# One transformer block on one core: the first attention layer in two halves of heads, its scores and softmax placed between pieces of the QKV and output products

## The chip, the core and the metric

One core of a Trainium2 chip runs the whole program. The metric is the device time of one execution in microseconds (us). Engines are named as the profile names them: PE is the matrix engine, DVE the vector engine, ACT the scalar engine, POOL the general one, SP the engine that here only issues DMAs. 1 MB is a million bytes.

## The reference, cut to what matters

Batch 1, 256 latent tokens and 256 context tokens, width 1024, everything in float32. The first layer is differential attention over 8 heads:

```python
sh1, sc1, g1, sh2, sc2, g2 = split(silu(c) @ w_mod[i] + b_mod[i], 6)     # 6 x 1024 columns, for two layers
hx, hc = x * (1 + sc1) + sh1, ctx * (1 + csc1) + csh1                    # csh1, csc1 from c_ctx
q, k, v = hx @ w_q, concat(hc, hx) @ w_k, concat(hc, hx) @ w_v           # w_qkv is 1024 x 3072
q, k_latent = rope(q), rope(k_latent)
p[h, m] = softmax(q[h, m] @ k[h, m].T / 8)                               # 8 heads, m = 0, 1, 256 queries x 512 keys
o[h] = (p[h, 0] - lam * p[h, 1]) @ v[h]                                  # 128 wide
y = (rms(o[h]) * subln_g * (1 - lam_init)) @ w_o                         # 1024 x 1024
x = layer_norm(ALPHA * x + g1 * y)
x = layer_norm(ALPHA * x + g2 * swiglu(x * (1 + sc2) + sh2))             # "ffn0": 1024 x 5632, 2816 x 1024
```

A second layer (pooling, then "ffn1") and a third block ("z", three sparse attentions, "ffn2") follow. The change doesn't touch what they compute.

## The kernel before, in words

**Weight panels.** All big weights go through one list, `w_panels` (L124): pieces of 512 rows by 512 columns, 1.05 MB each. SP issues the DMA of panel i into a ring of four slots (L1873 to L1882) once panel i-4 has been used (`sp.wait_ge(*done[i - RING])`). To reach float32 accuracy each panel is split: ACT writes its rounded high part (`split_hi`, L858) into one of two buffers, so it must wait until panel i-2 has been used, and DVE writes the low part (`split_lo`, L1114). `split_to(n)` on either engine works through the panels up to n, in order. PE then makes three products for each tile (high by high, high by low, low by high; `product`, L493).

The order is qkv (12 panels, 0 to 11), wo (12 to 15), ffn0_in (16 to 37, two for each of 11 column blocks "nb"), ffn0_out (38 to 49), pool (50), ffn1_in (51 to 72), and so on.

**The modulation.** `w_mod` is two layers of 1024 x 6144. The kernel takes it in 24 pieces ("events") of 512 columns, 2.1 MB each, into two buffers of `aux` (`mod_panel`, L389). Events 0 to 3 (shift and scale of the first layer, needed at once) are made on PE as 8 products of 2 columns by 512. Events 4 to 23 are made on DVE (`mod_product`, L1195): one tensor_scalar and seven scalar_tensor_tensor of 128x512 each, and PE only sums over partitions (`mod_reduce`). `mod_acc` counts finished DVE events. The DMA of event e overwrites the buffer of event e-2, so SP waits for `mod_acc` before it issues it. SP is one queue: a panel DMA that stands behind such a wait waits too. Where the mod DMAs stand among the panels is worked out in L1869 to L1872:

```python
at = min(event_panel[e - 4] + (5 if e < 16 else 7), event_panel[e - 2] + 3)
```

In ffn0_in there are six events for 11 column blocks (`FFN_EVENTS`: nb 1, 3, 5, 7, 9, 10), and four in ffn0_out (`OUT_EVENTS`).

**First attention layer.** (1) Prologue: constants, 16 small loads and the table, all on SP's queue; the four PE events; transposes of x. (2) QKV in six column blocks (`gemm`, L512), 2 or 4 token tiles each, Q and K by tokens; DVE turns Q and K by the rope tables in four instructions for each tile (L1253 to L1258). The transposes and the modulation of the context stand behind the first block. (3) Q and K are transposed by PE and copied back (L537, L911, L1267). (4) 16 units (token tile, head): two score products (K = 64 each, two row halves of the array), maxima on DVE (two reductions and a scaling, L1273, L1275), two exponentials on ACT (L924), mixing on DVE (four instructions, L1282 to L1289), four transposes on PE, a copy on ACT (L933), four value products on PE. Three units are in flight. (5) Norm of the heads, eight transposes, the wo product (four groups of 24 tiles' products), then residual and LayerNorm (`residual_stats`, L1332; `normalise`), and ffn0.

**In ffn0_in**, DVE does for block nb: low part of panel p(nb,0)+2, the second half of an event of nb-1, low part of p(nb,1)+2, then multiply, round and subtract for the block's activations, then finish an event and start the next (L1424 to L1446).

## Time and profile before

| what | us |
|---|---|
| median of 3 runs | 1356.54 (1355.19 to 1358.63) |
| the profiled execution's own time | 1360.89 |
| its span, first to last instruction | 1359.1 |
| PE busy / DVE busy / ACT busy | 1197.0 / 851.9 / 493.5 |
| first QKV product starts | 63.6 |
| first ffn0_in product starts | 311.6 |
| mean granted PE clock | 0.947 of full |

All times in a trace count from the span's start. The profiled execution took 4.4 us more than the median, 1.8 us of it outside the span. "Idle before, with a releaser" is time in which an engine stood still, and the thing whose semaphore ended it. A busy share says little by itself: PE's ends are modelled, and each stage has its own limit.

### The profile page before, as it was taken

Reading aid. Unit: us, or ns where it says so; the run is one execution under the profiler, and the core shown is the slowest. Engines: PE = TensorE matmul, PEld = TensorE weight load, DVE = VectorE, ACT = ScalarE, POOL = GpSimd, SP = SyncE. Lnnn points to the kernel's source line nnn. Section 1 sums busy time; section 2 is a strip of 40 time slices with the busy share of each in tenths; the row PEclk is TensorE's granted clock in tenths of the full one; section 3 lists DMA queues with packets and bytes.
Section 4 is the critical chain, followed back from the end, with each engine's and each line's share of the span. In section 5 each row is a group of like instructions: output and inputs, shape, how many; then the busy total and the mean of one; then the engine's idle time right before and its main releaser. Section 6 shows DMA issues by size and latency. Waiting matters only on the chain.

```text
span 1359.1 us, 17055 instructions
## 1 busy us (share of the span) xinstructions
PE 1197.0 (88%) x6927; PEld 1006.6 (74%) x6927; DVE 851.9 (63%) x1304; ACT 493.5 (36%) x688; POOL 90.3 (7%) x33
## 2 busy tenths in 40 slices
PE   4779997679999887799999699949999898899998
PEld 0257775469999675699987598847787646799977
DVE  0388858866878877755554665767856425555543
ACT  0232226534333222333333445524444333433332
POOL 0000000000000000000000002321224200000000
PEclk9889999999999898799999799968889999899999
DMA  6967687154887674485555356511122244455553
GB/s 214 361 229 266 229 294 167 32 201 125 274 291 254 236 263 136 133 288 184 181 175 173 107 182 202 155 32 63 34 73 80 79 138 153 126 185 182 180 181 109
DMA packets 155758, 236.77 MB, mean 174 GB/s; under 512 B 4901, under 2 KB 86178, under 8 KB 155554
## 3 DMA queue, kind: packets, MB, share of 16 engines
q1 hardware_dynamic: 150068, 223.36, 49.4%
q10 hardware_dynamic: 5614, 12.33, 3.3%
q8 instruction: 55, 0.90, 0.3%
q14 instruction: 21, 0.17, 0.0%
HBM read 229.12 MB, written 6.55 MB: 173 GB/s over the span
## 4 chain that ended last, share of the span: by engine, by line
PE 69%; DVE 12%; issue 9%; ACT 4%; DMA 3%; POOL 1%; SPq 1%; POOLq 0%; DVEq 0%; ACTq 0%
PE bank L493 66%; PE bank L537 3%; ACT w_hi L858 2%; DVE ring_lo L1114 2%; DMA ring<-in_ffn_w_in 2%; DVE small L1273 1%; DVE modacc L1211 1%; POOL small L1807 1%; DMA aux<-in_w_mod 1%; SPq L1861 1%; POOL ring_lo L1798 1%; DVE y_tok L1352 1%; DVE small L1355 1%; DVE small L1682 1%; DVE y_tok L1349 1%
## 5 line engine op out<-in xcount | busy, mean ns | idle before, releaser
L1114 DVE TENSOR_TENSOR ring_lo<-ring,w_hi 128x2048 fp32r<-128x2048 f32 (+4 forms) x142 | 314.0, 2213 | 304.7 <-ACT w_hi L858 304.6
L858 ACT ACTIVATE w_hi<-ring 128x2048 fp32r<-128x2048 f32 (+4 forms) x154 | 285.9, 1858 | 560.7 <-PE bank L493 547.1
L493 PE MATMUL bank<-h_hi,w_hi 128*128 128x256 f32 x1056 | 303.2, 287 | 2.9 <-DVE h_lo L1133 1.9
L493 PE MATMUL bank<-h_lo,w_hi 128*128 128x256 f32 x1056 | 299.9, 284 | 0.0
L493 PE MATMUL bank<-h_hi,ring_lo 128*128 128x256 f32 x1056 | 299.7, 284 | 0.0
L493 PEld LDWEIGHTS bank<-h_hi,w_hi 128*128 128x128 f32 x1056 | 203.9, 193 | 5.5 <-issue 5.5
L493 PEld LDWEIGHTS bank<-h_lo,w_hi 128*128 128x128 f32 x1056 | 203.8, 193 | 1.7 <-issue 1.7
L493 PEld LDWEIGHTS bank<-h_hi,ring_lo 128*128 128x128 f32 x1056 | 203.8, 193 | 0.0
L493 PE MATMUL bank<-w_hi,h_hi 128*128 128x512 f32 (+4 forms) x416 | 168.7, 405 | 15.1 <-ACT big L906 4.8
L493 PE MATMUL bank<-ring_lo,h_hi 128*128 128x512 f32 (+4 forms) x416 | 164.7, 396 | 0.0
L493 PE MATMUL bank<-w_hi,h_lo 128*128 128x512 f32 (+4 forms) x416 | 164.0, 394 | 0.0
L493 PE MATMUL bank<-w_hi,ff_hi 128*128 128x512 f32 x264 | 105.3, 399 | 13.8 <-DVE ring_lo L1114 13.7
L493 PEld LDWEIGHTS bank<-w_hi,h_hi 128*128 128x128 f32 x416 | 82.1, 197 | 35.9 <-issue 18.9
L1211 DVE SCALAR_TENSOR_TENSOR modacc<-aux,cs,modacc 128x512 f32<-128x512 f32 x140 | 105.2, 752 | 4.8
L493 PE MATMUL bank<-big 128*128 128x128 f32 (+5 forms) x386 | 88.3, 417 | 20.3 <-ACT big L933 11.2
L493 PE MATMUL bank<-ring_lo,ff_hi 128*128 128x512 f32 x264 | 104.4, 396 | 0.0
L493 PE MATMUL bank<-w_hi,ff_lo 128*128 128x512 f32 x264 | 104.3, 395 | 0.0
L493 PEld LDWEIGHTS bank<-w_hi,h_lo 128*128 128x128 f32 x416 | 81.8, 197 | 16.0
L493 PEld LDWEIGHTS bank<-ring_lo,h_hi 128*128 128x128 f32 x416 | 81.9, 197 | 14.6 <-issue 0.2
L493 PEld LDWEIGHTS bank<-big 64*128 64x128 f32 (+2 forms) x386 | 55.3, 209 | 46.1 <-issue 26.0
L1807 POOL TENSOR_TENSOR small<-small,neghalf 128x2 f32<-128x2 f32 (+1 forms) x11 | 16.8, 1531 | 873.7 <-DVE small L1360 481.3
L537 PE MATMUL bank<-table,y_tok 128*128 128x128 f32 x128 | 26.3, 371 | 50.8 <-DVE y_tok L1374 27.3
(202 smaller groups left out, 1385.5 us busy)
## 6 DMA issues: line engine op xcount, KB each, us to landing
aux<-in_w_mod SPq DMA_DIRECT2D x24, 2048.0 KB, 10.0
ring<-in_ffn_w_in SPq DMA_DIRECT2D x88, 512.0 KB, 4.9
ring<-in_w_in SPq DMA_DIRECT2D x24, 1024.0 KB, 5.0
ring<-in_w_ffn_in SPq DMA_DIRECT2D x44, 512.0 KB, 4.7
ring<-in_ffn_w_out SPq DMA_DIRECT2D x20, 1024.0 KB, 5.2
ring<-in_attn_w_qkv SPq DMA_DIRECT2D x12, 1024.0 KB, 12.0
ring<-in_w_ffn_out SPq DMA_DIRECT2D x10, 1024.0 KB, 5.1
bias_rows<-srow ACTq DMA_DIRECT2D x1, 5376.0 KB
```

Of the source, the lines that this page charges most:

```text
L493: return nc.tensor.matmul(o, l, r, start=start, stop=stop, **kw)
L537: ins = nc.tensor.transpose(bank[0:src.shape[1], i * P:i * P + src.shape[0]], src, ident[0:src.shape[0], 0:src.shape[0]])
L858: nc.scalar.activation(panel_part(i, 0), raw_panel(i), ACT.Copy).then_inc(w_hi, 1)
L1114: V.tensor_tensor(panel_part(i, 1), raw_panel(i), panel_part(i, 0).bitcast(F32), ALU.subtract)\
L1211: ins = V.scalar_tensor_tensor(acc, w[:, j, :], c, acc, ALU.mult, ALU.add)
L1273: step(V.tensor_reduce(small[:, s + 4 + m:s + 5 + m], result(dve, ("S", u, m))[:, :], AX, ALU.max))
L1349: empties(V.tensor_tensor(y, result(dve, (stage, nb, tt))[:, :], gate[:, sl], ALU.mult), (stage, nb, tt))
L1352: step(V.scalar_tensor_tensor(y, x_tok[:, tt, sl], ALPHA, y, ALU.mult, ALU.add))
L1355: step(V.bn_stats(st, y))
L1682: V.tensor_scalar(small[:, o:o + 3], small[:, o + 8:o + 11], 0.1 * NEG, -1.0, ALU.max, ALU.mult)\
L1798: nc.gpsimd.tensor_tensor(panel_part(i, 1), raw_panel(i), panel_part(i, 0).bitcast(F32), ALU.subtract).then_inc(w_lo_mix, 1)
L1807: nc.gpsimd.tensor_tensor(dst, src, exponent, ALU.pow).then_inc(rstd_done, 1)
```

## The change

QKV runs as K, Q, V of heads 0 to 3, then K, Q, V of heads 4 to 7 (`QKV_ORDER`). K and Q are made transposed (weights as the stationary operand, 512 or 256 tokens moving), so their 48 transposes fall away; the rope's swap of halves becomes a product with a permutation (`swap`), and DVE turns two heads at once with three instructions. Latent and context tokens are modulated together in 512-wide chunks, the first four chunks ahead of the first product, the other four inside it. Scores of heads 0 to 3 stand between the value pieces, their transposes and value products between the K pieces of heads 4 to 7; those of heads 4 to 7 between pieces of wo. Maxima are one reduction over two banks, mixing three instructions. The four PE events use `cs[:, 2j:2j+32]` and write to four groups of 32 output partitions. The small loads move to ACT's queue. The remaining modulation is 20 halves (4 of 8 rows of a whole 1024-column component, 2.1 MB each): six in the attention, one in each of ffn0_in's blocks nb 0 to 9, two in ffn0_out, two in ffn1_in. The DMA of half m waits for products 0 to m-2 and stands ahead of panel 2m+6 for m = 8 to 15. The store of the bias rows (5.5 MB, ACT's queue) moves from behind QKV into the prologue, and the load of the bias from ffn1_in's block 2 to block 6.

```diff
+QKV_ORDER = (2, 0, 4, 3, 1, 5)
...
-    for nb in range(6):
+    for nb in QKV_ORDER:
         for kg in range(2):
             add(("qkv", nb, kg), a["attn_w_qkv"][0], kg, PK, nb * NB, nb * NB + NB)
-    for nb in range(2):
-        for kg in range(2):
+    for kg in range(2):
+        for nb in range(2):
...
+        modhalf = [v3(aux[:, 4096 * i:4096 * i + 4096], KC // 2) for i in range(MODS)]
...
-        turn = {"gemm": 0, "misc": 0, "unit": 0, "mix": 0}
-        POOLS = {"gemm": (0, 1, 2, 3, 4, 5), "misc": (6, 7), "unit": (0, 1, 2, 3, 4), "mix": (5,)}
+        POOLS = {"gemm": (0, 1, 2, 3, 4, 5), "misc": (6, 7), "unit": (0, 1, 2, 3, 4), "mix": (5,),
+                 "dense": (0, 1, 2, 3), "pre": (4, 5, 6, 7), "score": (4, 5, 6, 7), "out": (4, 5)}
...
+        FIRST = (0, 2, 1, 3)
+        N_FIRST, N_HALVES = 4, 20
+        def mod_first_panel(eng, n):
+            if n >= MODS:
+                result(eng, ("modrow", n - MODS))
+            e = FIRST[n]
+            eng.dma_start(modring[n % MODS], a["w_mod"][0, :, e * NB:(e + 1) * NB]
+                          .rearrange("(p j) n -> p j n", j=KC)).then_inc(mod_landed[n % MODS], 16)
+        def mod_half_panel(eng, m):
+            if m < MODS:
+                result(eng, ("modrow", N_FIRST - MODS + m))
+            else:
+                eng.wait_ge(mod_acc, m - MODS + 1)
+            l, comp = divmod(2 + m // 2, 6)
+            j0 = (m % 2) * (KC // 2)
+            rows = a["w_mod"][l, :, comp * D:(comp + 1) * D].rearrange("(p j) n -> p j n", j=KC)
+            eng.dma_start(modhalf[m % MODS], rows[:, j0:j0 + KC // 2, :]).then_inc(mod_landed[m % MODS], 16)
+        def mod_is_row(comp):
+            return comp in (2, 5, 6, 7, 8, 11)
+        HALF_AT = {("ffn0", nb): [6 + nb] for nb in range(10)}
+        HALF_AT.update({("ffn0_out", 0): [16], ("ffn0_out", 1): [17], ("ffn1", 1): [18], ("ffn1", 2): [19]})
+        COMP_AT = {("ffn0", 2): 5, ("ffn0", 4): 6, ("ffn0", 6): 7, ("ffn0", 8): 8, ("ffn0", 10): 9, ("ffn1", 4): 11}
...
+            def mod_rows_first(n):
+                pe.wait_ge(mod_landed[n % MODS], 16 * (n // MODS + 1))
+                bank = take(("modrow", n), "pre")
+                for j in range(KC):
+                    q = 32 * (j % 4)
+                    ins = mm(bank[q:q + 32, :], cs[:, 2 * j:2 * j + 32], modring[n % MODS][:, j, :], j < 4, j >= 4)
+                fills(ins, ("modrow", n))
...
+            def swap_keys(pr):
+                for h in (2 * pr, 2 * pr + 1):
+                    wait_emptied(pe, ("K", h))
+                pe.wait_ge(turn_landed, 16)
+                fills(mm(v3(take(("swapK", pr), "misc"), 2), swap, kT[:, 2 * pr:2 * pr + 2, SEQ:], True, True), ("swapK", pr))
...
+            def keys_and_queries(hg, between):
+                for kg in range(2):
+                    for j in range(4):
+                        keys(hg, kg, j)
+                        between(4 * kg + j)
+                queries(hg, 0)
+                between(8)
+                swap_keys(2 * hg)
+                swap_keys(2 * hg + 1)
+                queries(hg, 1)
+            def values_and_scores(hg):
+                vals(hg, 0, 0)
+                swap_queries(2 * hg)
+                swap_queries(2 * hg + 1)
+                if hg == 0:
+                    mod_sums(2)
+                vals(hg, 0, 1)
+                for u in range(6):
+                    scores(8 * hg + u)
+                    vals(hg, (u + 2) // 4, (u + 2) % 4)
+                for u in (6, 7):
+                    scores(8 * hg + u)
...
+            def first_columns(i):
+                if i == 1:
+                    for n in (2, 3):
+                        mod_rows_first(n)
+                if i == 2:
+                    for n in (2, 3):
+                        mod_columns_first(n)
+                    for ch in range(PK, KC):
+                        tokens(ch)
+                if i == 3:
+                    wait_emptied(pe, ("pre", KC - 1))
+            def first_heads(i):
+                if 1 <= i <= 8:
+                    values(i - 1)
+                if i < 8:
+                    turn_probs(i)
+                if i == 8:
+                    mod_sums(3)
+            wait_emptied(pe, ("pre", PK - 1))
+            keys_and_queries(0, first_columns)
+            values_and_scores(0)
+            keys_and_queries(1, first_heads)
+            values_and_scores(1)
...
+            o_transposes(0)
+            turn_probs(8)
+            turn_probs(9)
+            wait_emptied(pe, ("oT", 1))
+            wo(0, 0, 0)
+            values(8)
+            for u in range(9, 12):
+                turn_probs(u + 1)
                 values(u)
-
-
-            pe.wait_ge(o_done, 4)
-            for h in range(HEADS):
-                transposes(("oT", h), [y_tok[:, tt, h * P:(h + 1) * P] for tt in range(TT)])
+            wo(0, 0, 1)
+            for u in range(12, 16):
+                if u < 15:
+                    turn_probs(u + 1)
+                values(u)
+            wo(1, 0, 0)
+            mod_sums(4)
+            wo(1, 0, 1)
+            o_transposes(1)
+            wait_emptied(pe, ("oT", 3))
             for nb in range(2):
-                gemm("wo", lambda tt, c: token_tile(hT, c, tt), range(TT), nb, NB, HALVES,
-                     inputs=lambda c: (("oT", c),))
+                for tt in range(TT):
+                    wo(nb, 1, tt)
...
+            act.dma_start(table[:, :], a["const_table"]).then_inc(table_landed, 16)
+            for dst, src in small_loads:
+                act.dma_start(dst, src).then_inc(cols_landed, 16)
+            act.dma_start(lam_in, a["attn_lambda"][0].partition_broadcast(P)).then_inc(lam_landed, 16)
+            act.dma_start(big[:, 11776:12160], a["const_turn"]).then_inc(turn_landed, 16)
...
+            def scores_out(hg):
+                first = panel_at[("qkv", 4 + hg, 0)]
+                for u in (0, 1):
+                    exps(8 * hg + u)
+                split_to(first + 2)
+                for u in (2, 3):
+                    exps(8 * hg + u)
+                for tt in range(4):
+                    value_copy(hg, tt)
+                    if tt == 3:
+                        split_to(first + 3)
+                    exps(8 * hg + 4 + tt)
+            split_to(2)
+            for h in range(4):
+                key_copy(h)
+            split_to(4)
+            query_copy(0)
+            query_copy(1)
+            split_to(5)
+            scores_out(0)
+            for u in range(3):
+                probs_copy(u)
+            split_to(8)
+            probs_copy(3)
+            key_copy(4)
+            squares(0)
+            probs_copy(4)
+            key_copy(5)
+            probs_copy(5)
+            key_copy(6)
+            probs_copy(6)
+            key_copy(7)
+            split_to(9)
+            probs_copy(7)
+            split_to(10)
+            squares(1)
+            query_copy(2)
+            query_copy(3)
+            split_to(11)
+            scores_out(1)
+            o_highs(0)
+            for u in range(8, 12):
+                probs_copy(u)
+            squares(2)
+            split_to(14)
+            for u in range(12, 16):
+                probs_copy(u)
+            squares(3)
+            bias_row(g2row, 0, 5, g_landed[5])
+            for r, w in enumerate(("ln_g", "ln_b")):
+                row_load(ln_rows[:, r, :], a[w][0, 0, :], ln_landed)
+            split_to(15)
+            o_highs(1)
...
+            def mod_product(m, js=range(KC // 2)):
...
+                w = modhalf[m % MODS]
                 for j in js:
+                    jj = (m % 2) * (KC // 2) + j
+                    c = cs[:, 2 * jj:2 * jj + 1]
+                    if jj == 0:
+                        ins = V.tensor_scalar(modacc_raw[:, :], w[:, j, :], c, None, ALU.mult)
                     else:
                         settle()
+                        if j == 0:
+                            dve.wait_ge(mod_acc, m)
+                        ins = V.scalar_tensor_tensor(modacc_raw[:, :], w[:, j, :], c, modacc_raw[:, :], ALU.mult, ALU.add)
+                    if j < KC // 2 - 1:
                         step(ins)
                     else:
                         ins.then_inc(mod_acc, 1)
...
+            def turn_pair(kind, pr):
+                buf = (kT[:, 2 * pr:2 * pr + 2, SEQ:] if kind == "K" else qT[:, 2 * pr:2 * pr + 2, :])
+                t = v3(tmp[:, 0, :], 2)
+                if pr == 0 and kind == "K":
+                    dve.wait_ge(turn_landed, 16)
+                if pr == 2 and kind == "K":
+                    dve.wait_ge(sq_done, 2)
+                sin2 = rope_sin.unsqueeze(1).broadcast_to([P, 2, SEQ])
+                cos2 = rope_cos.unsqueeze(1).broadcast_to([P, 2, SEQ])
+                settle()
+                empties(V.tensor_tensor(t, v3(result(dve, ("swap" + kind, pr))[:, :], 2), sin2, ALU.mult), ("swap" + kind, pr))
+                step(V.tensor_tensor(buf, buf, cos2, ALU.mult))
+                wait_emptied(dve, ("swap" + kind, pr))
+                settle()
+                V.tensor_tensor(buf, buf, t, ALU.add).then_inc(rope_done, 1)
+                ropes[0] += 1
+                dve.wait_ge(rope_done, ropes[0])
...
+            def maxima_and_mixes(hg):
+                first = panel_at[("qkv", 4 + hg, 0)]
+                maxima(8 * hg)
+                for u in range(1, 8):
+                    maxima(8 * hg + u)
+                    combine(8 * hg + u - 1)
+                    if u == 2:
+                        split_to(first + 2)
+                    if u == 7:
+                        split_to(first + 3)
+                combine(8 * hg + 7)
+            mod_product(0)
+            split_to(2)
+            mod_product(1)
+            split_to(3)
+            turn_pair("K", 0)
+            split_to(4)
+            turn_pair("K", 1)
+            split_to(5)
+            turn_pair("Q", 0)
+            turn_pair("Q", 1)
+            mod_finish(2)
+            maxima_and_mixes(0)
+            mod_product(2)
+            split_to(8)
+            mod_product(3)
+            head_var(0)
+            head_norm(0)
+            split_to(9)
+            head_var(1)
+            split_to(10)
+            head_norm(1)
+            mod_finish(3)
+            turn_pair("K", 2)
+            turn_pair("K", 3)
+            mod_product(4)
+            split_to(11)
+            turn_pair("Q", 2)
+            turn_pair("Q", 3)
+            maxima_and_mixes(1)
+            o_lows(0)
+            mod_product(5)
+            head_var(2)
+            head_norm(2)
+            split_to(14)
+            mod_finish(4)
             head_var(3)
             head_norm(3)
-            lows("oT", hT, None, lambda ch: cols[:, COL_SUB:COL_SUB + 1])
-
-            def residual_stats(stage, gate, used, events={}, late=lambda: None):
+            split_to(15)
+            o_lows(1)
...
-                    for e in FFN_EVENTS[name].get(nb - 1, []):
-                        mod_product(e + 2, range(PK, KC))
+                    for m in HALF_AT.get((name, nb - 1), []):
+                        mod_product(m, range(KC // 4, KC // 2))
...
+                        mod_finish(COMP_AT[(name, nb)])
+                    for m in HALF_AT.get((name, nb), []):
+                        mod_product(m, range(KC // 4))
...
+            def out_products(nb):
+                split_to(panel_at[("ffn0_out", nb, 1)] + 2)
+                for m in HALF_AT[("ffn0_out", nb)]:
+                    mod_product(m)
+            residual_stats("ffn0_out", g2row, g2_used, out_products)
+            mod_finish(10)
+            fold_norm(6, 1)
...
+            mod_first_panel(sp, 0)
+            mod_first_panel(sp, 1)
             sp.dma_start(x_tok, a["x"][0].rearrange("(t p) d -> p t d", p=P)).then_inc(x_landed, 16)
             sp.dma_start(y_tok, a["ctx"][0].rearrange("(t p) d -> p t d", p=P)).then_inc(ctx_landed, 16)
-            row_load(lam_in, a["attn_lambda"][0], lam_landed)
-            mod_panel(sp, 2)
-            mod_panel(sp, 3)
-
-            mods_before = {RING: [4, 5], 5: [6], 6: [7]}
-            for e in range(8, N_EVENTS):
-                at = min(event_panel[e - 4] + (5 if e < 16 else 7), event_panel[e - 2] + 3)
-                mods_before.setdefault(at, []).append(e)
+            halves_before = {RING: [0, 1], 6: [2], 7: [3], 11: [4], 12: [5], 15: [6], 17: [7]}
+            for m in range(8, N_HALVES):
+                halves_before[{16: 40, 17: 43, 18: 50, 19: 52}.get(m, 2 * m + 6)] = [m]
             for i, (key, srcs, chunks, width) in enumerate(panels):
-                for e in mods_before.get(i, []):
-                    mod_panel(sp, e)
+                for m in halves_before.get(i, []):
+                    mod_half_panel(sp, m)
+                if i == 1:
+                    mod_first_panel(sp, 2)
+                if i == 2:
+                    mod_first_panel(sp, 3)
```

## Rows read from the trace of the kernel before

**Rows 1.** Busy time by stretch: from:to, length, PE, PEld, DVE, ACT, POOL, clock, DMA, GB/s

```profile
0.00:63.60 63.60, 36.41 (x101) 9.08 (x102) 10.89 (x32) 10.07 (x17) 0.21 (x4) 0.98 0.81 285
63.60:206.50 142.90, 128.09 (x554) 102.85 (x554) 112.58 (x153) 41.23 (x48) 0.00 (x0) 0.94 0.73 258
206.50:276.30 69.80, 50.65 (x303) 34.46 (x304) 57.76 (x141) 39.70 (x98) 4.04 (x4) 0.95 0.39 85
276.30:311.60 35.30, 25.44 (x112) 20.70 (x110) 23.26 (x35) 12.37 (x16) 2.68 (x1) 0.90 0.55 193
311.60:438.90 127.30, 126.95 (x1031) 124.41 (x1032) 97.94 (x103) 47.25 (x36) 0.00 (x0) 1.00 0.74 245
438.90:522.00 83.10, 72.73 (x331) 59.80 (x330) 67.40 (x80) 22.16 (x14) 0.00 (x0) 0.94 0.69 241
...
693.10:756.30 63.20, 60.08 (x264) 49.10 (x262) 31.05 (x23) 23.11 (x14) 0.00 (x0) 1.00 0.54 181
```

**Rows 2.** Chain that ended last, prologue to ffn0: start, length, what

```profile
57.08 0.91 ACT h_hi L868 x2
...
127.55 22.04 PE bank L493 x96
...
301.88 0.29 DVE small L1358 x2
...
311.64 33.48 PE bank L493 x272
```

**Rows 3.** PE in order of time, one event, last wo product: start, length, form

```profile
40.14 7.03 PE L493 MATMUL bank<-aux,cs 128*2 128x512 f32 x16 [1.59 <-DMA aux<-in_w_mod]
...
297.67 0.39 PE L493 MATMUL bank<-w_hi,h_lo 128*128 128x512 f32 x1
```

**Rows 4.** PE in order of time, attention units

```profile
224.02 0.60 PE L537 MATMUL bank<-table,prob 128*128 128x128 f32 x4
224.55 1.13 PE L493 MATMUL bank<-big 64*128 64x512 f32 x4
226.53 1.16 PE L493 MATMUL bank<-big 128*128 128x128 f32 x8 [0.85 <-ACT big L933]
```

**Rows 5.** Groups of DVE instructions, shapes apart: total busy, mean ns, idle before

```profile
L1114 DVE TENSOR_TENSOR ring_lo<-ring,w_hi 128x2048 fp32r<-128x2048 f32 x128 | 292.9, 2290 | 277.7 <-ACT w_hi L858 277.6
L1211 DVE SCALAR_TENSOR_TENSOR modacc<-aux,cs,modacc 128x512 f32<-128x512 f32 x140 | 105.2, 752 | 4.8
...
L1273 DVE TENSOR_REDUCE small<-bank 128x1 f32<-128x512 f32 x32 | 20.5, 683 | 2.4 <-PE bank L493 2.3
...
L1380 DVE SCALAR_TENSOR_TENSOR x_tok<-y_tok,small,aux 128x1024 f32<-128x1024 f32 x2 | 2.6, 1279 | 0.0
```

**Rows 6.** Busy time by stretch, columns as in rows 1: DMA rates, a cold restart

```profile
50.00:52.00 2.00, 2.00 (x6) 0.39 (x5) 0.00 (x0) 0.00 (x0) 0.00 (x0) 1.00 1.05 389
...
461.60:465.60 4.00, 3.94 (x9) 3.15 (x10) 3.93 (x5) 0.00 (x0) 0.00 (x0) 0.50 0.99 354
```

**Rows 7.** SP's queue in order of time, ffn0_in: start, length, what

```profile
349.58 0.55 SPq L397 DMA_DIRECT2D aux<-in_w_mod  x1
...
374.38 0.56 SPq L397 DMA_DIRECT2D aux<-in_w_mod  x1
```

**Rows 8.** Chain that ended last, one panel of ffn0_in

```profile
354.42 12.59 DMA ring<-in_ffn_w_in
...
367.08 1.93 ACT w_hi L858
...
369.04 2.30 DVE ring_lo L1114
```

**Rows 9.** DMA issues at 31.4 and at 377.5: count, KB each, us to landing

```profile
aux<-in_w_mod SPq DMA_DIRECT2D x1, 2048.0 KB, 8.7
...
ring<-in_ffn_w_in SPq DMA_DIRECT2D x2, 512.0 KB, 8.3
```

**Rows 10.** DMA issues of the whole span: count, KB each, median us to landing

```profile
ring<-in_ffn_w_in SPq DMA_DIRECT2D x88, 512.0 KB, 4.9
```

623 lines of the change are left out of this document (324 added, 299 removed).

## The prediction

> **What bounds the kernel now.** I read the busy time by stretch first, then the chain of waits, then PE in order of time, DVE's groups with shapes apart, and last the DMA issues with their landing times. By stretch [rows 1]: ffn0_in is full of PE work (126.95 of 127.3 us), the first 311.6 us are not. Before the first QKV product PE is busy 36 of 63.6 us, in attention 51 of 69.8 us while DVE has 58, between wo and ffn0 25 of 35.3 us, in ffn0_out 73 of 83.1 us. ffn1_out, the same products without modulation in between, takes 63.2 us [rows 1]. So some 75 us stand open before ffn0 and some 20 in ffn0_out. DVE's group for low parts has 278 us of idle time ended by ACT's high part [rows 5]. So the split follows PE (each high part needs the buffer of two panels ago), with little slack in a panel of 5.8 us (127.3 / 22).
>
> **Up to the first product, part by part.** The loads needed are two mod pieces (4.2 MB), x and ctx (2.1), and table and small ones (0.8 in all): 7.1 MB at 354 to 389 GB/s [rows 6] with some 2 us to start is 20 to 22 us; I take 22. Their order no longer puts the table behind 4 MB. Then four chunks on ACT, twelve instructions of about 0.46 us [rows 2], 5.6 us, the high part of panel 0 (1.93 [rows 8]) and its low part (2.3): first product at 33 us, before 63.6.
>
> One unknown is in there, the four column groups. Before, one event is 16 records in 7.03 us [rows 3]. Ends: no overlap, 7.0 us an event; full overlap, 1.8. I take about 2.5, since the row of the scores shows overlap of this kind: two products of 512 columns on two row halves take 1.13 us [rows 4] where two in turn would be 1.76 (2 x 7.03 / 8). The first two events lie beside the loads of x and ctx; the other two are on PE's path, 5 us. The Trainium skill, "TensorE: Matmul & The Clock Gate", Part 3, gives 2.38 times for three column tiles, which would be 3 us an event; the sum would be 1 us longer.
>
> **From there to ffn0.** PE's work: 20 groups of 24 products, at 0.23 each (22.04 / 96 [rows 2]) 110 us, with 1 us more for the queries' 256 columns; wo 22; 16 units of 1.13 for scores, 0.53 for transposes (to the next start) and 1.0 to 1.16 for values [rows 4], 43; eight products with the permutation at 0.88, 7; modulation sums, events 2 and 3, and remaining transposes, 17. Together 199 us, so 232 if PE never waits. DVE has 148 us in this time: 15 low parts at 2.29, six halves at 5.1 (four times 1.28, the 1024-wide row), 16 units of 1.25 for one maximum over 1024 elements (two 512-wide ones take 0.68 each) and 1.25 for mixing, eight turns of 2.1 (three instructions of about 0.7), norms and low parts of activations. So DVE isn't the bound; its order makes PE wait in places. I followed the three programs against each other with these durations and find: 2.3 us ahead of the second half of K (chunks 4 to 7), 2.8 after the Q permutations (two banks are freed by DVE's turns), 2.1 at the second pair of K permutations (a bank waits for the head norm), 5.3 after the last scores (transposed heads 0 to 3 wait for the mixing of the last unit) with 1.8 for a cold restart, 2.2 where ACT's high part of panel 14 stands ahead of a copy of probabilities, 3.5 ahead of wo's second half and some 6 in small ones and restarts: 24 us. Wo ends at 256. The last wo product before ended at 298 [rows 3], and 13.6 us later ffn0 began [rows 2]. That stretch grows by 2.4, because the low part of panel 16 now comes ahead of the first residual rows. With 1.5 for the column groups, ffn0 begins at 273 instead of 311.6: **38.6 us less**. Ends: 249 if all waits vanish, 297 if they double. The bias store (5.5 MB) now lies beside QKV loads that have 10 us of slack and more; I cost it at 0.
>
> **ffn0_in, where I expect it back.** The new order of DMAs makes a closed chain, once for each column block. SP may issue half m only when product m-2 has ended. Panel 2m+6 stands behind it on SP. The second part of product m-1 stands on DVE behind the low part of that same panel. And half m+1 waits for that product. So a round is: half and panel to landing, high part, low part, two instructions of product, next half. It must fit in PE's 11.5 us for two panels (127.3 / 11 [rows 1]).
>
> Its price from rows. A 2.1 MB mod transfer issued into an idle queue lands after 8.7 us [rows 9]; 1.05 MB more at 389 GB/s [rows 6] is 2.7: 11.4 us, the lower end. Upper: at 349.58 SP issued a mod transfer [rows 7], and the panel behind it landed at 354.42 + 12.59 = 367.0 [rows 8], 17.4 us later; three row loads of ACT (1.6 MB, 4.2 us) were among them, which leaves 13.2. The second case, issued at 374.38 [rows 7], with its panel at 377.5 landing 8.3 later [rows 9], is 11.4. I take 12.3, the middle, since the next panel's transfer follows at once and shares the engines. With 1.93 and 2.30 [rows 8], 2.6 for two 1024-wide instructions [rows 5] and 0.2 for semaphores a round is 19.3 us (18.4 to 20.2), 7.8 more than PE's 11.5. Before, an event came every second block (23 us), so the same chain fitted.
>
> The first half in it (m = 8) is issued some 13.2 us after block 0 ends: 4.2 for the low part, 1.8 for activations, 2.2, 2.3, 2.6. Panel 22 is then ready at 29.8, PE wants it at 23.0: 6.8 us. Seven rounds follow, to panel 36: 7 x 7.8 = 54.6. ACT's row loads fall into one of them, 4. Sum **65 us more** (54 to 73). DVE's own load, 6.2 + 5.2 + finishing in each block, is hidden in these rounds.
>
> **ffn0_out and the rest.** Four events of up to 6 us on DVE (eight instructions, 0.75 each [rows 5]) become two halves of 5.1. ffn0_out took 83.1 - 63.2 = 20 us longer than ffn1_out [rows 1]; of it I leave 5 (PE's sums over partitions, about 2 us, two low parts 0.8 late, one 1.8 late): **15 less** (12 to 18). mod_finish(10) and the fold now stand behind the residual, 0.7, and ffn1 takes two halves in its first blocks: **2 more** together (0 to 4). The bias load at ffn1's block 6 collides as it did at block 2: 0.
>
> **Sum.** -38.6 + 65 - 15 + 2 = +13.4 us against the profiled execution's 1360.9 (span 1359.1), so 1374.3; that execution stood 4.4 above the median, and against 1356.5 it is **1370 us**. With its bounds the case runs from 1352 to 1386.
>
> **The rivals.**
>
> *The panel overtakes the half* (faster). Place: the transfer of panel 2m+6. Where no mod transfer is ahead, a panel's pieces land in 4.9 us [rows 10]. If they did so here, a round would be 4.9 + 0.6 of issue + 7.0 = 12.5, one us over PE's time, so about 8 us in all: -38.6 + 8 - 15 + 2 = -44, 1313 us. It decides from a landing of about 4.5 us downward that nothing waits. Against it: the 12.59 us of rows 8. The Trainium skill, "DMA: Bandwidth & Descriptors", Queues, rings and completion order, says that descriptors start in ring order but that completion is not first in, first out; by the second part this rival would have its chance, by the first the forecast stands. 0.12.
>
> *Attention gives more than the chain takes.* If nearly all the 24 us of waits vanish (PE far enough ahead) and a round is at its lower end, it is -58 + 54 - 17 + 2 = -19, 1338 (39 and 20 of the 24 gone; 65 less 11). Half way there the two sides cancel, within 4 us of before. For it: my list of waits is long, and each is worked out from an order that may slide. 0.25 for both.
>
> *The column groups run in turn.* An event stays at 7.0 us. The second one ends at 31 instead of 22, and 9 us go on the path; events 2 and 3 cost 14 instead of 5. With the sum: 1370 + 18 = 1388. Against it: the overlap in rows 4. 0.1.
>
> *PE's cold clock joins the chain.* After a wait of 5 us PE ran at 0.50 of its clock (1.2 GHz) for 4 us and made 9 products in it [rows 6], instead of some 17. In each round PE waits 7.8 us, so each block would start slow and take 2 us more. It would decide if PE's panel were on the chain; but the high part of panel 2m+8 needs only panel 2m+6 used, 8 us into a round of 19. Were it on it, 8 x 2 = 16 us more, 1386. 0.03. The Trainium skill, "TensorE: Matmul & The Clock Gate", HAM oscillation, warns of just such waits between bursts; by it alone the 1386 would stand.
>
> The forecast keeps 0.5. About 0.3% (4 us) is what a measurement of this kernel can tell from no change. Faster by more: 0.12 and half of the second rival, 0.25 in all. Within: 0.13. Slower: 0.62. The range for 8 in 10 reaches from the second rival's end to a little past the third: 1338 to 1390.
>
> **What would show it.** Right: first product near 33 us, first ffn0_in product at 265 to 281; PE idle 6 to 9 us ahead of every second panel from the fourth block of ffn0_in, ended by DVE's low part, that by ACT's high part, that by the landing; SP waiting for DVE's modacc ahead of each mod transfer; granted clock in ffn0_in below 1.00; ffn0_out near 68 us. Wrong: low parts in ffn0_in 5.8 us apart throughout, with panels landing in 5 us behind a mod transfer (then the first rival), or ffn0 beginning before 260 (the second), or an event of column groups taking 7 us (the third).

## The result, and the profile after

The changed kernel takes **1375.94 us** (median of 4 runs, 1373.72 to 1380.11), before beside it 1356.16: ratio 1.0147, 95% interval 1.0118 to 1.0176. The profiled execution took 1374.82 (span 1373.0) against 1360.89 (1359.1). By the medians the change costs 19.8 us, by the two profiled executions 13.9, since before's stood 4.4 above its median and after's 1.1 below. The forecast was 1370. Between the first products of the stages the two profiles differ so:

| from ... to | before | after | difference | forecast |
|---|---|---|---|---|
| start to first QKV product | 63.6 | 35.6 | -28.0 | -30.6 |
| to first ffn0_in product | 248.0 | 252.3 | +4.3 | -8.0 |
| to first ffn0_out product | 133.2 | 186.2 | +53.0 | +65 |
| to the pool's first product | 87.4 | 75.0 | -12.4 | -15 |
| from there to the end | 826.9 | 823.9 | -3.0 | +2 |

Busy time by stretch of after (columns as in [rows 1]):

```profile
0.00:33.00 33.00, 11.27 (x69) 5.37 (x69) 9.35 (x41) 10.22 (x17) 0.20 (x4) 0.96 0.97 346
...
36.00:60.00 24.00, 20.51 (x112) 14.64 (x111) 8.75 (x16) 7.38 (x13) 0.00 (x0) 0.90 0.90 332
...
215.00:230.00 15.00, 8.37 (x35) 6.97 (x34) 13.59 (x18) 7.64 (x14) 0.00 (x0) 0.66 0.17 66
230.00:272.00 42.00, 34.42 (x194) 29.22 (x192) 13.92 (x23) 12.31 (x14) 2.02 (x2) 0.92 0.64 225
272.00:288.00 16.00, 3.80 (x17) 3.19 (x18) 13.10 (x23) 5.29 (x11) 2.68 (x1) 0.68 0.21 66
288.00:475.50 187.50, 148.44 (x1091) 138.51 (x1092) 132.05 (x122) 50.17 (x37) 0.00 (x0) 0.90 0.67 233
475.50:549.00 73.50, 62.81 (x278) 51.24 (x276) 44.26 (x43) 19.37 (x11) 2.68 (x1) 0.94 0.69 243
```

In [rows 1] ffn0_in was the stage without idle PE time; now PE stands still for some 39 of its 187.5 us, at a mean clock of 0.90. The DMA share fell from 0.74 to 0.67: more bytes, but not at a higher rate. PE in order of time (start, length, form, idle before it and what ended that):

```profile
35.62 0.77 PE L525 MATMUL bank<-hc_hi,w_hi 128*128 128x512 f32 x1 [8.67 <-DVE ring_lo L1360]
...
43.67 3.64 PE L525 MATMUL bank<-aux,cs 128*32 128x512 f32 x32
...
60.02 0.50 PE L525 MATMUL bank<-hc_hi,w_hi 128*128 128x512 f32 x1 [3.52 <-DVE hc_lo L1459]
...
172.88 2.05 PE L525 MATMUL bank<-big 128*128 128x512 f32 x2 [4.02 <-DVE modcol L1505]
...
257.59 0.80 PE L525 MATMUL bank<-w_hi,h_hi 128*128 128x512 f32 x1 [4.35 <-DVE h_lo L1600]
...
287.92 0.36 PE L525 MATMUL bank<-h_hi,w_hi 128*128 128x256 f32 x1 [1.05 <-DVE h_lo L1379]
...
330.38 3.78 PE L525 MATMUL bank<-modacc,ones 128*128 128x512 f32 x4 [7.67 <-DVE modacc L1481]
...
403.88 3.78 PE L525 MATMUL bank<-modacc,ones 128*128 128x512 f32 x4 [9.22 <-DVE modacc L1481]
```

The row at 43.67 answers to the first of [rows 3]: two events in 3.64 us, 1.82 each, where one took 7.03. The last two are PE's waits for the halves' products: four such waits (7.67 us at 330.38, 8.72 at 367.60, 9.22 at 403.88, 8.14 at 439.63), one in two blocks, each ahead of a sum over partitions, and a fifth of 3.95 at the end of the stage. PE waited for the low part of a panel only once, 1.35 us at 347.1. The chain of waits of after, one round of ffn0_in (the longest of eight, 19.2 us; three row loads of ACT, issued from 326.4 to 327.3, landed in it):

```profile
330.36 0.37 SPq L435
...
330.77 0.51 SPq L2188
...
331.32 11.34 DMA ring<-in_ffn_w_in
...
342.74 1.92 ACT w_hi L1029
...
344.69 2.29 DVE ring_lo L1360
346.98 1.21 DVE modacc L1481
...
348.21 1.30 DVE modacc L1481
349.53 0.37 SPq L435
```

This is the closed chain link by link, where [rows 8] showed the same links after a normal panel: SP issues the half (L435), the panel behind it (L2188), its landing, high part, low part, the previous half's two instructions, and SP's next half. No PE row is in it. On SP's queue, in order of time, eight rounds lie between these two issues of halves, 17.7 to 19.2 us long, 18.1 in the mean:

```profile
312.47 0.37 SPq L435 DMA_DIRECT2D aux<-in_w_mod  x1
...
457.41 0.37 SPq L435 DMA_DIRECT2D aux<-in_w_mod  x1
```

From the page, the groups of instructions that answer to [rows 5] (busy, mean ns, idle before), and the DMA issue that answers to [rows 10]:

```profile
L1360 DVE TENSOR_TENSOR ring_lo<-ring,w_hi 128x2048 fp32r<-128x2048 f32 (+4 forms) x142 | 314.3, 2214 | 328.6 <-ACT w_hi L1029 328.6
...
L1481 DVE SCALAR_TENSOR_TENSOR modacc<-aux,cs,modacc 128x1024 f32<-128x1024 f32 x70 | 89.8, 1283 | 1.7
...
ring<-in_ffn_w_in SPq DMA_DIRECT2D x88, 512.0 KB, 5.8
```

The wider products cost what [rows 5] had for a 1024-wide instruction (1283 ns for 1279). The median landing of a piece rose from 4.9 to 5.8 us.

### The profile page after: what moved, and what is told of

It reads as the page before. It is cut to its first block, busy times and chain, and to the rows that moved or that the text cites. A ratio compares the mean times of both kernels' runs of the same rounds, so it can differ in the third digit from the quotient of the medians.

```text
span 1373.0 us, 17100 instructions
## 1 busy us (share of the span) xinstructions
PE 1189.5 (87%) x7007; PEld 1011.6 (74%) x7007; DVE 819.4 (60%) x1163; ACT 489.8 (36%) x676; POOL 92.3 (7%) x33
## 4 chain that ended last, share of the span: by engine, by line
PE 62%; DVE 13%; issue 9%; DMA 7%; ACT 5%; POOL 2%; SPq 1%; ACTq 1%; POOLq 0%; DVEq 0%
PE bank L525 59%; DMA ring<-in_ffn_w_in 7%; DVE ring_lo L1360 4%; ACT w_hi L1029 3%; DVE modacc L1481 3%; PE bank L567 3%; POOL small L2133 1%; SPq L2188 1%; POOL ring_lo L2124 1%; DVE small L2008 1%; DVE y_tok L1669 1%; DVE small L1672 1%; ACT hc_hi L1078 0%; ACTq L1061 0%; DVE y_tok L1666 0%
## 5 line engine op out<-in xcount | busy, mean ns | idle before, releaser
L525 PE MATMUL bank<-w_hi,h_hi 128*128 128x512 f32 (+4 forms) x320 | 130.5, 408 | 10.1 <-DVE h_lo L1600 4.4
L525 PE MATMUL bank<-ring_lo,h_hi 128*128 128x512 f32 (+4 forms) x320 | 126.4, 395 | 0.0
L525 PE MATMUL bank<-w_hi,h_lo 128*128 128x512 f32 (+4 forms) x320 | 125.9, 393 | 0.0
L1481 DVE SCALAR_TENSOR_TENSOR modacc<-aux,cs,modacc 128x1024 f32<-128x1024 f32 x70 | 89.8, 1283 | 1.7
L525 PE MATMUL bank<-big 64*128 64x128 f32 (+5 forms) x274 | 77.4, 483 | 11.9 <-issue 7.8
L525 PEld LDWEIGHTS bank<-w_hi,h_hi 128*128 128x128 f32 x320 | 63.7, 199 | 25.5 <-issue 8.8
L525 PEld LDWEIGHTS bank<-w_hi,h_lo 128*128 128x128 f32 x320 | 63.3, 198 | 12.1
L525 PEld LDWEIGHTS bank<-ring_lo,h_hi 128*128 128x128 f32 x320 | 63.6, 199 | 10.4
L567 PE MATMUL bank<-table,y_tok 128*128 128x128 f32 x124 | 25.1, 359 | 49.0 <-DVE y_tok L1691 30.5
L525 PEld LDWEIGHTS bank<-big 64*128 64x128 f32 (+2 forms) x274 | 42.1, 214 | 30.6 <-issue 26.2
```

Of the source, the lines that this page charges most:

```text
L525: return nc.tensor.matmul(o, l, r, start=start, stop=stop, **kw)
L567: ins = nc.tensor.transpose(bank[0:src.shape[1], i * P:i * P + src.shape[0]], src, ident[0:src.shape[0], 0:src.shape[0]])
L1481: ins = V.scalar_tensor_tensor(modacc_raw[:, :], w[:, j, :], c, modacc_raw[:, :], ALU.mult, ALU.add)
```

## The experiments

All ratios are to the kernel before, run beside them on the same chip. "ffn0_in" is the time from its first product to the first ffn0_out product: 133.2 before, 186.2 after.

**1. The half one panel later.**

```diff
-                halves_before[{16: 40, 17: 43, 18: 50, 19: 52}.get(m, 2 * m + 6)] = [m]
+                halves_before[{16: 40, 17: 43, 18: 50, 19: 52}.get(m, 2 * m + 7)] = [m]
```

> The changed kernel, with the DMA of half m (m = 8 to 15) put ahead of panel 2m+7 instead of 2m+6. Bytes, DVE's work and its order stay. Theory, a closed chain (half m issued, panel 2m+6 behind it 11.3 us later, high part 1.9, low part 2.3, product of half m-1 2.6, half m+1; 18.1 us a round against PE's 11.5): the panel whose low part releases half m+1 no longer stands behind half m, so the chain is open. What is left is DVE's own load, 129 us for 11 blocks (22 low parts 51, ten halves 51, 22 for the activations, 5 to finish), so ffn0_in takes 130 to 140 us instead of 187.6 and the whole 1318 to 1330. Rival, the 2.1 MB beside each two panels are too much for the DMA queue or the low parts are late through bandwidth: rounds stay near 18 us and the whole above 1360. Rival, PE's cold clock carries the chain on: rounds stay above 14 us, the whole above 1335.

1342.81 us, ratio 0.9884 (0.9856 to 0.9913), ffn0_in 150.5. One number takes away two thirds of what the stage had lost, with the same bytes and the same work: the chain is the cause, and runs 2 to 4, at three other links, bear it out. But 13 to 25 us of the expected gain are missing. The first rival doesn't fit. The second has its time (the whole is above 1335) but not its rounds (13.4 us in the steady part, below 14) and not its cause: the granted clock in ffn0_in is 0.99. PE's waits stand where they stood in after, ahead of the five sums and ended by DVE's product, but they are 1.8 to 3.9 us long. The chain of waits of this kernel says what came in its place:

```profile
350.87 1.30 DVE modacc L1481
...
352.21 13.51 PE bank L525 x100
365.74 1.92 ACT w_hi L1029
367.69 0.03 DVE ring_lo L1360
367.72 2.17 issue
369.90 0.69 DVE tmp L1750
...
371.68 1.29 DVE modacc L1481
...
373.00 1.28 DVE modacc L1481
374.28 2.20 DVE ring_lo L1360
376.48 1.21 DVE modacc L1481
...
377.71 1.30 DVE modacc L1481
...
379.05 13.51 PE bank L525 x100
```

This is a second closed loop, over two blocks: PE's sum over partitions (once for two halves) waits for the odd half's product; PE then makes the sum and a block (13.5 us); only then is the buffer free for the high part (1.9), low part (2.2), activations (2.0), product (2.6), low part (2.2), product (2.6), and the next sum. 26.8 us for two blocks, where two PE blocks and a sum are some 25. It was hidden behind the first loop's 36.

**2. The same link cut on DVE.**

```diff
+                    for m in HALF_AT.get((name, nb - 1), []):
+                        mod_product(m, range(KC // 4, KC // 2))
                     split_to(panel_at[(name + "_in", nb, 0)] + 2)
-                    for m in HALF_AT.get((name, nb - 1), []):
-                        mod_product(m, range(KC // 4, KC // 2))
```

> The changed kernel, with the same link cut from DVE's side: in ffn0_in the second part of the product of half m-1 stands ahead of the low part of panel 2m+6, not behind it. The order of the DMAs stays. Theory of the closed chain: half m+1 no longer waits for a low part whose panel stands behind half m; ffn0_in takes 130 to 140 us, the whole 1318 to 1330. Rival, the order on SP's queue alone is the cause (a panel behind a 2.1 MB transfer is late, whoever waits for it): the panels still land 11 us after the half, rounds stay at 18 us, the whole within 5 us of 1375.

1340.84 us, ratio 0.9871 (0.9841 to 0.9901), ffn0_in 152.5. SP's order is the one of after and the time falls as in run 1. So the late panel alone costs little; it is the ring from it back to the next half that costs. The profiled execution took 1347.83, 7 us more than the median, so its 152.5 may be high. The rest expected is missing here too. PE's six waits (12.0 us together, the longest 5.0) are now all for low parts; that DVE has both parts of a product, the finish and the activations between two low parts would explain them, but no run tests it.

**3. Half the bytes, and 4. another link shorter by 1.3 us.**

```diff
-            eng.dma_start(modhalf[m % MODS], rows[:, j0:j0 + KC // 2, :]).then_inc(mod_landed[m % MODS], 16)
+            n = KC // 4 if 8 <= m < 16 else KC // 2
+            eng.dma_start(modhalf[m % MODS][:, 0:n, :], rows[:, j0:j0 + n, :]).then_inc(mod_landed[m % MODS], 16)
```

> The changed kernel, with the DMAs of halves 8 to 15 cut to half their bytes (1.05 MB): half of the rows of these eight halves of w_mod are left out, and the products read old data in their place. The order of everything stays. Theory of the closed chain: the landing of the panel behind the half comes 2.7 us sooner (1.05 MB at 389 GB/s), a round is 15.4 instead of 18.1, eight rounds give 19 to 24 us, the whole 1351 to 1356. Rival, DVE's load or the products' length sets the round: no change, 1370 to 1378. Rival, landing times are all latency and queueing: under 1 us a round, above 1367.

1358.46 us, ratio 1.0001 (0.9981 to 1.0020), ffn0_in 169.3: 17 us less, a round is 15.9 instead of 18.1 (issues from 315.02 to 441.98). Most of the 2.7 us of transfer time comes off each round, not all; the whole lies 2.5 us above the expected range's upper end, 8.5 below the nearer rival.

```diff
-                        mod_product(m, range(KC // 4, KC // 2))
+                        mod_product(m, range(KC // 4 + 1, KC // 2))
-                        mod_product(m, range(KC // 4))
+                        mod_product(m, range(KC // 4 + 1))
```

> The changed kernel, with each half's product in ffn0_in cut 3 and 1 instructions instead of 2 and 2: three at the end of a block, one behind the next block's first low part. DVE does the same work, SP issues in the same order. Theory of the closed chain: the link from low part to the next half's issue is one 1024-wide instruction (1.3 us) shorter, a round is 16.8 instead of 18.1, eight rounds give 10 us, the whole 1362 to 1368. Rival, DVE's total load sets the pace: no change, 1372 to 1379.

1366.59 us, ratio 1.0067 (1.0041 to 1.0093), rounds of 17.0 (314.12 to 450.20 in eight), ffn0_in 178.2: 8 us less with DVE's work unchanged. Time taken off a link, on DMA or on DVE, comes off the round: 2.2 of an expected 2.7 us in run 3, 1.1 of 1.3 in run 4.

**5. One column group in the prologue.**

```diff
-                    q = 32 * (j % 4)
-                    ins = mm(bank[q:q + 32, :], cs[:, 2 * j:2 * j + 32], modring[n % MODS][:, j, :], j < 4, j >= 4)
+                    ins = mm(bank[0:32, :], cs[:, 2 * j:2 * j + 32], modring[n % MODS][:, j, :], j == 0, j == KC - 1)
```

> The changed kernel, with the four modulation events of the prologue on one group of 32 output partitions instead of four: the same 8 products of 32 columns by 512 an event, the sum over j made in one group. Theory, the four groups run beside each other (1.8 us an event at full clock, four times less than the 7.0 of one in turn): an event takes 7.0 us again; events 0 and 1 put 9 on the path to the first product, events 2 and 3 ten more inside the first K products, less what lies beside loads: 14 to 20 us longer, 1389 to 1395. Rival, the gain of the prologue comes from the order of the loads alone: within 4 us of 1375.

(The sum over partitions behind it then reads these 32 partitions alone.) 1395.26 us, ratio 1.0275 (1.0247 to 1.0303): 19 us by the medians, 17 by the two ratios, in the expected range. PE in order of time shows both places:

```profile
16.55 16.41 PE L525 MATMUL bank<-aux,cs 128*32 128x512 f32 x32
...
45.39 0.77 PE L525 MATMUL bank<-hc_hi,w_hi 128*128 128x512 f32 x1 [8.66 <-DVE ring_lo L1359]
```

The first K product comes at 45.39 instead of 35.62 (+9.8), the first ffn0_in product at 306.5 instead of 287.9 (+18.6). So the groups carry 10 of the 28 us of the prologue, and had the third rival come true, the kernel would have taken 1395 instead of that rival's 1388.

**6. Half the product, on top of run 1.**

```diff
-                        mod_product(m, range(KC // 4, KC // 2))
+                        mod_product(m, range(KC // 2 - 1, KC // 2))
-                        mod_product(m, range(KC // 4))
+                        mod_product(m, range(1))
```

> The kernel with half m ahead of panel 2m+7, in which each part of a product in ffn0_in makes one instruction instead of two: half of the rows of these ten halves of w_mod are left out of the sums. All bytes are still loaded. What held ffn0_in at 150.5 us (first product to first ffn0_out product) there, where before took 133.2? Theory, DVE: PE's sum over partitions at the end of every second block waits for the product's second part, which stands behind a low part (high 1.9, low 2.2, product 2.6 after PE's mid-block is 6.7 us against PE's 5.8), and the panel behind that sum stands still with it. With 1.3 for the part it is 5.4: ffn0_in 133 to 136, the whole 1325 to 1330. Rival, the bytes (44 MB in 150 us) or the landing of the panels behind halves: ffn0_in stays above 145, the whole above 1337.

1329.65 us, ratio 0.9795 (0.9769 to 0.9821), ffn0_in 141.1: the whole is in its range, the stage is above the 133 to 136 expected and below the rival's 145. The waits ahead of four of the five sums are gone, so DVE's stretch is what made them and not the bytes. Of the 8 us over before's 133.2, 3.5 are PE's own (five sums of 1.9 us, 1024 columns each, where before had six of 1.0), 2.4 a wait at 344.3 behind a panel that landed 16.3 us after its issue (beside ACT's three row loads), and 1.3 a wait at the last sum.

**7. mod_finish(3) ahead of panel 10's low part, and 8. the bias store late.**

```diff
             head_var(1)
+            mod_finish(3)
             split_to(10)
             head_norm(1)
-            mod_finish(3)
```

> The changed kernel, with mod_finish(3) ahead of the low part of panel 10 and the norm of the second heads on DVE, instead of behind them. The wait of 4.0 us at 172.9 (PE's second permutation of K pair 3, for a bank that mod_finish(3) empties) goes: the finish can run at 168.6 instead of 172.6. Theory: it is on PE's path, 4 us less in all, 1370 to 1373. Rival, it comes back at the next wait (the turns of Q, or the last scores at 215): under 1.5 us, 1374 to 1377.

1374.29 us, ratio 1.0124 (1.0104 to 1.0143): not told apart from after's 1.0147 (1.0118 to 1.0176), and by its time in the rival's range, not the theory's. Its profile tells more: the wait of 4.02 at 172.88 is gone, and a new one stands further on, at the turns of Q, where the rival put it; the second row's was there before (5.76 at 220.79 in after):

```profile
186.41 1.13 PE L525 MATMUL bank<-big 64*128 64x512 f32 x4 [2.92 <-DVE big L1541]
...
218.26 1.94 PE L567 MATMUL bank<-table,y_tok 128*128 128x128 f32 x8 [5.75 <-ACT tmp L1117]
```

and ffn0_in begins 2.7 us sooner (285.24), but takes 188.1 instead of 186.2. So two thirds of the gain reached ffn0, and there most of it was lost again in that one execution; why the stage took 1.9 longer isn't settled.

```diff
-            act.wait_ge(srow_done, 1)
-            act.dma_start(scratch, srow[:, :].unsqueeze(1).broadcast_to([REL_HEADS, P, SROW])).then_inc(srow_stored, 16)
...
             o_highs(0)
+            act.wait_ge(srow_done, 1)
+            act.dma_start(scratch, srow[:, :].unsqueeze(1).broadcast_to([REL_HEADS, P, SROW])).then_inc(srow_stored, 16)
```

> The changed kernel, with the 5.5 MB store of the bias rows moved from the prologue to behind the last scores on ACT's queue. Theory (costed at 0 in the forecast): the QKV panels beside it have slack, within 2 us of 1375. Rival, the store shares the DMA engines with panels 1 to 5 (QKV panels land 13 us after their issue in the profile of after): PE's waits before 92 us shrink, 3 to 8 us less, 1367 to 1372. Third, the store lies beside wo's panels now and costs there: 2 to 6 us more.

1376.36 us, ratio 1.0143 (1.0122 to 1.0164): no change. The DMA issues from 33 to 90 us of after, and of this kernel:

```profile
ring<-in_attn_w_qkv SPq DMA_DIRECT2D x5, 1024.0 KB, 17.1
```

```profile
ring<-in_attn_w_qkv SPq DMA_DIRECT2D x5, 1024.0 KB, 8.3
```

The store doubles the landing time of five QKV panels and costs nothing: they have that slack. Nor does a cost behind wo hide a gain: PE's eleven waits behind the first K product, up to ffn0, are those of after, each within 0.03 us. The forecast's 0 holds.

**9 to 12. Toward a version that beats both.** Run 9 took half 6 out of ffn0_in, on top of run 1, with the other halves, the sums and the DMAs one block earlier; run 10 added run 7's edit and a cut of 3 and 1 for odd halves.

```diff
             o_lows(1)
+            mod_product(6)
...
-        HALF_AT = {("ffn0", nb): [6 + nb] for nb in range(10)}
+        HALF_AT = {("ffn0", nb): [7 + nb] for nb in range(9)}
```

> The kernel with half m one panel later, and besides the whole product of half 6 on DVE between the last low parts of the attention and the wo residual, where DVE stands still for 9.8 us (257.9 to 267.6 in the profile of after). Halves 7 to 15 move one block earlier, each half ahead of panel 2m+5; ffn0_in holds nine instead of ten. Theory, DVE's stretches between PE's stages and its sums are what is left in ffn0_in (150.5 us there): one block of eleven has no product, the last sum's wait of 3.9 and the stall behind the first mod transfers shrink, ffn0_in 143 to 147, the whole 1334 to 1339. Rival, the product delays the wo residual or the ffn0 activations (ffn0 starts later by more than 2 us): the whole 1340 to 1345.

> The same, with mod_finish(3) moved ahead as in the run of that alone (ffn0 began 2.7 us sooner there) and the odd halves' products cut 3 and 1 (their second part, on which PE's sum waits, 1.3 us shorter). Theory: the attention's gain is now kept, since no chain behind it sets ffn0_in's end, and each of the four or five sums waits some 1.2 us less while DVE's stretch ahead of a low part grows by 1.3 and costs under 1: 4 to 6 us less than the one before it, 1328 to 1334. Rival, the longer stretch costs what the sums give: 1332 to 1337.

1344.48 us, ratio 0.9880 (0.9852 to 0.9907), and 1343.15, ratio 0.9855 (0.9827 to 0.9884). Both miss their ranges. Run 9's time is in its rival's range, but not by the rival's cause (ffn0 starts 1.4 us later than in run 1, not over 2); run 10 is outside its rival's too. ffn0_in takes 154.1 and 154.5, though DVE has less to do. The sums tell why it doesn't fall. In runs 1, 9 and 10 alike they come 26.8 us apart in the steady part; here those of run 10:

```profile
368.94 1.98 PE L525 MATMUL bank<-modacc,ones 128*128 128x512 f32 x4 [1.90 <-DVE modacc L1481]
...
395.79 1.98 PE L525 MATMUL bank<-modacc,ones 128*128 128x512 f32 x4 [1.84 <-DVE modacc L1481]
```

I had read the wait ahead of a sum as one part of a product (2.6 us) behind a low part. It is the loop that decides, and in it both parts of the odd half lie in a row: 2+2 or 3+1, one block earlier or later, it is as long. Why the stage is 4 us longer than run 1's isn't shown; the first two gaps between sums are some 28 us in both, where run 1 has one such, and the granted clock 0.97 and 0.96 where run 1 has 0.99. So the place of PE's sum has to change (run 11, on top of runs 1 and 7, with the even halves cut 1 and 3):

```diff
+                        if kg == 1 and (name, nb - 1) in COMP_AT:
+                            mod_sums(COMP_AT[(name, nb - 1)])
                         w = panel((name + "_in", nb, kg))
...
-                    if (name, nb) in COMP_AT:
-                        mod_sums(COMP_AT[(name, nb)])
+                if (name, FNB - 1) in COMP_AT:
+                    mod_sums(COMP_AT[(name, FNB - 1)])
```

> The kernel with half m ahead of panel 2m+7, with mod_finish(3) moved ahead, and in the ffn stages PE's sum over partitions half a block later (ahead of the next block's second panel instead of behind the block); the even halves' products are cut 1 and 3. In the runs with ten or nine halves and with 2+2 or 3+1 the sums came 26.8 us apart whatever was moved: PE from the sum through the next block 13.5, high part 1.9, low part 2.2, activations 2.0, both parts of the odd product 5.2, a low part 2.2, and then the sum again. Theory of this second loop: half a block of PE work (5.8 us) now lies beside DVE's part of it, the waits of 12.4 us ahead of the five sums go, and DVE waits up to 2 us for the sum ahead of each even product instead, which costs PE 0.5 to 2 us in every second block: ffn0_in 140 to 146 instead of 150.5, with 2 us of the attention the whole 1331 to 1337. Rival, DVE's own work is the bound there (131 of 151 us busy) and the waits only change places: ffn0_in 148 or more, the whole 1338 to 1343.

1339.56 us, ratio 0.9870 (0.9837 to 0.9903), ffn0_in 148.7: at the rival's times. Yet by stretch the profile has the steady part as the theory wants it, PE busy all the time in three of the first four stretches:

```profile
311.00:335.00 24.00, 24.00 (x192) 23.04 (x191) 22.10 (x21) 7.86 (x6) 0.00 (x0) 1.00 0.92 329
335.00:363.00 28.00, 24.50 (x183) 23.37 (x182) 22.17 (x20) 8.62 (x6) 0.00 (x0) 0.94 0.97 340
363.00:387.00 24.00, 24.00 (x192) 23.04 (x191) 21.71 (x20) 8.63 (x6) 0.00 (x0) 1.00 0.96 335
387.00:411.00 24.00, 24.00 (x192) 23.04 (x192) 21.79 (x21) 8.62 (x6) 0.00 (x0) 1.00 0.96 336
411.00:436.00 25.00, 19.05 (x140) 18.50 (x140) 24.65 (x23) 6.71 (x5) 0.00 (x0) 0.86 0.78 279
```

Its sums come 24.7 us apart (357.12, 381.86, 406.61). What is left stands elsewhere: 3.5 us at 344.2 for the low part of a panel that landed 15.0 us after its issue, beside ACT's three row loads (issued from 323.5 to 324.3), and 5.0 ahead of the last sum,

```profile
432.16 3.58 PE L525 MATMUL bank<-ones,modacc 128*128 128x1 f32 x16 [5.00 <-DVE modacc L1483]
```

which stayed at the end of ffn0_in. Run 12 puts it behind ffn0_out's first panel:

```diff
+                    if (stage, nb, kg) == ("ffn0_out", 0, 0):
+                        mod_sums(9)
...
-                if (name, FNB - 1) in COMP_AT:
-                    mod_sums(COMP_AT[(name, FNB - 1)])
```

> The kernel before it, with the fifth sum (component 9) behind the first panel of ffn0_out on PE instead of at the end of ffn0_in, where PE waited 5.0 us at 432.2 and then ran at a cold clock. Theory: PE makes that panel's 24 products (5.5 us) in the time of the wait, DVE's finish comes no later; 4 to 6 us less, the whole 1333 to 1336. Rival, PE wants the low parts and activations that stand behind DVE's finish, and waits as long ahead of the next panel: under 2 us less, 1338 to 1340.

**1335.59 us, ratio 0.9839** (0.9813 to 0.9866), ffn0_in 142.8 (the last sum now counts to ffn0_out). By the two ratios it is 4 us less than run 11, as expected, though their intervals overlap; by the profiles the wait of 5.0 is gone, and one of 2.6 appears at 428.8, ahead of ffn0_out's first product:

```profile
428.84 0.47 PE L525 MATMUL bank<-w_hi,ff_hi 128*128 128x512 f32 x1 [2.57 <-DVE ring_lo L1362]
```

Without a product or a byte less, five edits of order turn the change from 1.5% slower than before into 1.6% faster.

## Why the prediction was right, point by point

The sign is right, and so is the cause of the loss, the closed chain in ffn0_in. The size agrees between the two profiled executions (forecast +13.4 us, measured +13.9); by the ratio of the medians the change costs 20 us (16 to 24), more than forecast. And the sum is better than its terms by luck, since two errors of some 12 to 15 us cancel. Its bounds, 1352 to 1386, don't follow from those of the terms either: with 38.6 fixed the others give 1354 to 1383, and attention's own ends, 249 and 297, would have made it far wider.

- **Up to the first product**: 35.6 for 33. ACT's first chunk started at 25.8, where my sum had 22 us for the loads; what follows took 9.9. Column groups: taken at 2.5 us an event, measured 1.82 for the last two (3.64 for both), the "full overlap" end; the first two took 5.28 together. Run 5 shows the groups worth 17 to 19 us in all. The Trainium skill, "TensorE: Matmul & The Clock Gate", Part 3, gives 2.38 times for three tiles; four groups gave 3.8 here (13.92 us for the two events in one group, 3.64 in four).
- **From there to ffn0: the term that was mis-sized.** "38.6 us less" measured 23.7, and ffn0 began at 287.9, outside the 265 to 281 that I had named as the sign of being right. Of the 14.9, 2.6 are the late first product; 12.5 lie between it and wo's end (271.1). PE's idle time between the first product and wo's end is 25.1 us against the 24 listed (which held some restarts too), and four of the listed waits are there within 2 us (3.5 at 60, 4.0 at 172.9, 5.8 at 220.8, 4.4 at 257.6). What failed is "PE's work: 199 us": it was summed with the 0.23 us of a warm stretch, and PE was busy for 210.4. The granted clock was 0.90 from 36 to 60 us, 0.66 from 215 to 230, 0.92 from 230 to 272. One group of PE's products from 33 to 272 us has a mean of 443 ns, where the last row of [rows 3] has 0.39 us for the same shape:

```profile
L525 PE MATMUL bank<-hc_hi,w_hi 128*128 128x512 f32 x64 | 28.4, 443 | 12.2 <-DVE ring_lo L1360 8.7 <-DVE hc_lo L1459 3.5
```

 Behind six waits, those that ended at 35.6, 60.0, 128.7, 172.9, 220.8 and 257.6 (2.15 to 8.67 us long), the granted clock was 0.50 to 0.65 for the next 4 to 5 us; behind the three of 0.9 to 2.1 us at 91.6, 93.7 and 239.9 it stayed at 1.00. I had priced one restart (1.8) and left the others to "some 6 in small ones and restarts". Busy time times what the clock lacked, over the stretches from 33 to 272, comes to some 14 us; that it is the whole excess is argued from rows, no run tests it. So the rebuilt attention by itself gave nothing from the first product on (+4.3, with two of the modulation events and the context's chunks moved into it); the gain is the prologue's.
- **ffn0_in**: the chain is there as written, shown by runs 1 to 4. PE's waits are not where I had put them: not 6 to 9 us ahead of every second panel, ended by a low part, but once in two blocks ahead of the sum, ended by the product (7.7 to 9.2 us). The first half was issued 24.6 us after the stage began (24.7 forecast). A round is 18.1 for 19.3: the panel landed 10.8 to 12.3 us after the half's issue, 11.3 in the mean of eight, at the lower end and not in the middle (12.3). And PE's block before was 12.1 us with its share of the sums (133.2 / 11), not 11.5: my stretch in [rows 1] ended at 438.9, with most of the last panel of ffn0_in still to come (its products end at 443.4), while the first ffn0_out product comes at 444.8. The round in which the row loads landed was 1.2 us longer (19.2, where the other seven have 18.0 in the mean), not 4. Counted from the trace, eight rounds at 6.0 over a block are 48, and the 41.2 us ahead of the first and behind the last issue are 5 more than three blocks: 53. On PE's side these are 38 us more of idle time, some 10 of slow clock and 3.5 of wider sums.
- **ffn0_out and the rest**: -12.4 for -15. The same boundary had put this stage's excess over ffn1_out at 20 us; from the first product to the last it was 16.5 (78.5 for 62.0), and 3.4 of it is left (65.5 for 62.1), where I had left 5. The +2 behind was -3.0, 2.5 of it in ffn1_in (131.4 before, 128.9 after), not looked into.
- **The rivals.** The panel did not overtake the half in any of the eight rounds; the landing of 11.34 us in the chain above is the row against it. Attention gave less than the sum had, not more. The column groups did not run in turn (1.82 us an event). Cold clock on the chain: after the waits PE ran slowly (a sum took 3.78 us instead of 1.9, at a granted clock of 0.50), but the chain has no PE row, and a round is the sum of its other links. The Trainium skill, "TensorE: Matmul & The Clock Gate", HAM oscillation, describes such restarts. The granted clock behind the waits agrees. By the rows of the chain they cost nothing in ffn0_in; before ffn0 they are, as argued above, what my sum lacked.
- **What I did not see**: the second loop behind the first (runs 1, 9, 10; run 11, which moves the sum, brings it from 26.8 to 24.7 us), since I counted DVE's load per block as "hidden in these rounds" and never followed PE's sum back to its own release of the buffer.

## What to carry to other kernels

When a transfer waits for work that stands behind a panel, and that panel stands behind the transfer, write the ring out and add up its links: it sets the pace if it is longer than the bound engine's time for one turn, however idle each engine is. Moving the transfer one panel back, or the work one place forward, opened it here without a byte or a product less. Then look for the next ring: shifting work from one part to another inside a ring that holds both left it as long. And price PE's waits with their slow restarts, where PE is on the path.
